# Expert weights read with eight neighbouring rows on a partition

## The reference, cut to what matters

```python
def routed_moe(x, router_w, router_b, w_gate, w_up, w_down):
    ...
    for e in range(N_EXPERTS):                       # 16
        h = jax.nn.silu(xt @ w_gate[e]) * (xt @ w_up[e])      # [512,1024] @ [1024,512]
        y = y + gates[:, e:e + 1] * (h @ w_down[e])           # [512,512] @ [512,1024]
    return y.reshape(B, S, D)
```

## Time and profile before

| | |
|---|---|
| median of 3 runs | 2137.74 us (2133.09 to 2142.99) |
| profiled execution, its own time | 2131.04 us |
| its span | 2129.4 us |
| mean granted TensorE clock | 0.945 of full |
| PE busy | 1977.8 us (93%) |
| weight loads (PEld) busy | 890.7 us (42%) |
| DVE / ACT / POOL busy | 671.2 / 402.5 / 82.1 us |
| moved by DMA | 335.56 MB in 140634 packets |

### The profile page before, as it was taken

How to read it: one execution, slowest core, us unless ns; L and a number is a source line. 1 busy time by engine, 2 the same in 40 slices (tenths; PEclk the granted TensorE clock), 3 DMA queues, 4 the chain that set the end, 5 groups by cost and what they waited for, 6 DMA issues and landing times.

```text
span 2129.4 us, 23221 instructions
## 1 busy us (share of the span) xinstructions
PE 1977.8 (93%) x9718; PEld 890.7 (42%) x9718; DVE 671.2 (32%) x1600; ACT 402.5 (19%) x869; POOL 82.1 (4%) x106
## 2 busy tenths in 40 slices
PE   7999999999999998997997999998999898899998
PEld 3454444444444444543544332333644445333322
DVE  4736312223200312105525100005586645200005
ACT  3213011111100013006501111112116421111112
POOL 0000010000000000000000200010000000200001
PEclk9989999999999999997796999999898997899999
DMA  4104542221212212201044899993110233699995
GB/s 156 60 21 142 193 159 79 79 79 69 79 40 79 79 53 79 79 4 37 1 150 152 295 399 398 396 393 138 40 40 1 80 132 145 193 397 396 397 386 206
DMA packets 140634, 335.56 MB, mean 158 GB/s; under 512 B 4537, under 2 KB 12745, under 8 KB 140401
## 3 DMA queue, kind: packets, MB, share of 16 engines
q1 hardware_dynamic: 126384, 283.80, 36.7%
q0 software_dynamic: 10976, 37.76, 4.7%
q10 hardware_dynamic: 3168, 12.50, 1.4%
HBM read 310.94 MB, written 23.09 MB: 157 GB/s over the span
## 4 chain that ended last, share of the span: by engine, by line
PE 79%; issue 8%; DMA 6%; DVE 5%; ACT 2%; POOL 0%; DVEq 0%; another core or an unknown queue 0%; ACTq 0%; POOLq 0%; SPq 0%
PE psum L580 32%; PE psum L978 20%; PE psum L823 7%; DMA ring<-in_moe_w_up 5%; PE psum L760 5%; PE psum L889 3%; PE psum L917 2%; PE psum L902 2%; PE psum L1072 1%; PE psum L959 1%; PE psum L702 1%; PE psum L592 1%; ACT ring L1429 1%; PE psum L1003 0%; PE psum L1095 0%
## 5 line engine op out<-in xcount | busy, mean ns | idle before, releaser
L978 PE MATMUL psum<-ring,scratch 128*32 128x512 f32 x3840 | 513.9, 602 | 14.4 <-DMA ring<-in_moe_w_up 11.4
L580 PE MATMUL psum<-xT,ring 128*128 128x512 f32 (+2 forms) x1056 | 466.1, 602 | 8.6 <-PE psum L580 3.4
L580 PEld LDWEIGHTS psum<-xT,ring 128*128 128x128 f32 (+2 forms) x1056 | 199.6, 191 | 272.5 <-issue 271.6
L978 PEld LDWEIGHTS psum<-ring,scratch 128*32 128x32 f32 x3840 | 142.5, 111 | 300.2 <-issue 296.0
L580 PE MATMUL psum<-ring,xT 128*128 128x512 f32 (+4 forms) x704 | 242.5, 501 | 2.5 <-ACTq L1181 1.6
L580 PEld LDWEIGHTS psum<-ring,xT 128*128 128x128 f32 x704 | 123.0, 199 | 120.1 <-issue 111.9
L823 PE MATMUL psum<-ring,scratch 128*128 128x512 f32 x352 | 155.7, 603 | 4.0 <-remote 3.3
L1591 DVE SCALAR_TENSOR_TENSOR scratch<-psum,overlay,scratch 128x511 f32<-128x511 f32 x88 | 65.9, 749 | 232.1 <-ACT scratch L1360 230.5
L978 PE MATMUL psum<-xT,scratch 128*32 128x512 f32 x768 | 129.1, 602 | 8.4 <-DMA ring<-in_moe_w_up 8.4
L2128 DVE TENSOR_TENSOR scratch<-psum,scratch 128x512 f32<-128x512 f32 x24 | 16.6, 692 | 335.9 <-PE psum L978 335.9
L823 PEld LDWEIGHTS psum<-ring,scratch 128*128 128x128 f32 x352 | 67.4, 193 | 91.6 <-issue 91.6
(11 more groups left out here) (374 smaller groups left out, 1647.3 us busy)
## 6 DMA issues: line engine op xcount, KB each, us to landing
ring<-in_moe_w_gate SPq DMA_DIRECT2D x28, 2048.0 KB, 15.1
ring<-in_moe_w_up SPq DMA_DIRECT2D x28, 2048.0 KB, 18.5
ring<-in_moe_w_down SPq DMA_DIRECT2D x24, 2048.0 KB, 16.0
ring<-in_w_up SPq DMA_DIRECT2D x11, 2048.0 KB, 7.9
xT<-in_moe_w_down SPq DMA_DIRECT2D x8, 2048.0 KB, 11.6
expert_rows<-scratch ACTq DMA_DIRECT2D x20, 512.0 KB, 7.5
ring<-in_w_down SPq DMA_DIRECT2D x4, 2048.0 KB, 7.7
ring<-in_even_w_in SPq DMA_DIRECT2D x4, 2048.0 KB, 7.7
```

The lines of the kernel that those rows point to most:

```text
L580: mm = nc.tensor.matmul(out_, lhsT, rhs, start=(j == 0), stop=(j == len(pairs) - 1))
L978: mm = nc.tensor.matmul(bank[r, :], lhsT[:, t, r], w_[:, t, c0:c0 + 512], start=(t == 0), stop=(t == nk - 1))
```

## The change

A partition now holds neighbouring rows of an expert's matrix: for gate and up partition p holds rows 8 p to 8 p + 7, for down rows 4 p to 4 p + 3. That is one unbroken piece of 16 KB in DRAM and in the buffer, and the load is written with two dimensions (128 x 4096) instead of three. The bytes in a buffer are read as before, [partition, k, n]; product k now takes the rows 8 p + k. So the turned operand must hold column 8 p + k of x on partition p: transpose k of `turn_x` reads every eighth element of a row (32 bytes apart), from k on, and transpose k of `turn_h` every fourth element of `hid` (16 bytes apart). Number, order and engine of all instructions, and all waits, stay as they were. The path for tokens beyond an expert's 96 places (`overflow`) keeps the old layout in both its loads and its transposes.

```diff
--- before.py
+++ after.py
@@ -953,11 +953,12 @@
                 mm.then_inc(idx_mm, 1)
 
             def turn_x(l, g):
+
+                of_partition = xg[:, g % 2, :].rearrange("q (p k) -> q k p", k=KD)
                 pe.wait_ge(gathered[g % 2], 16 * (NG // 2 * l + g // 2 + 1))
                 for h in range(2):
                     for t in range(4):
-                        mm = nc.tensor.transpose(banks[h][:, t * P:(t + 1) * P],
-                                                 xg[:, g % 2, (4 * h + t) * P:(4 * h + t + 1) * P], ident)
+                        mm = nc.tensor.transpose(banks[h][:, t * P:(t + 1) * P], of_partition[:, 4 * h + t, :], ident)
                     mm.then_inc(xgT_done, 1)
 
             def weights_of(l, m, g):
@@ -998,9 +999,10 @@
                     tiled(banks[5 + j], hidT, 4, views, j * 512).then_inc(y_done, 1)
 
             def turn_h(l, g):
+                of_partition = hid.rearrange("q (p k) -> q k p", k=4)
                 pe.wait_ge(h_ready, NG * l + g + 1)
                 for t in range(4):
-                    mm = nc.tensor.transpose(banks[4][:, t * P:(t + 1) * P], hid[:, t * P:(t + 1) * P], ident)
+                    mm = nc.tensor.transpose(banks[4][:, t * P:(t + 1) * P], of_partition[:, t, :], ident)
                 mm.then_inc(hT_done, 1)
 
             def share_late(l):
@@ -2532,7 +2534,7 @@
 
             def load_experts(l):
                 c0 = first_expert_chunk[l]
-                views = {m: w[n][l].rearrange("e (k p) n -> e p k n", p=P) for m, n in zip(("gate", "up", "down"), EXPERT_W)}
+                views = {m: w[n][l].rearrange("e (p k) n -> e p (k n)", p=P) for m, n in zip(("gate", "up", "down"), EXPERT_W)}
                 for m, e, b, freed in loads_of[l]:
                     if freed:
                         m_, g = freed
@@ -2548,7 +2550,8 @@
                         if b < 2:
 
                             sp.wait_ge(met, meets_through("odd_d" if l else "even_b"))
-                    sp.dma_start(expert_buffer(b, 4 if m == "down" else KD), views[m][e]).then_inc(expert_loaded[b], 16)
+
+                    sp.dma_start(expert_buffer(b, 1)[:, 0, :], views[m][e]).then_inc(expert_loaded[b], 16)
 
             for at, c in static:
                 if at < first_expert_chunk[0]:
```

## The result

| | before | after |
|---|---|---|
| median | 2135.41 us (2130.12 to 2142.99, 4 runs) | 2109.39 us (2109.26 to 2114.14, 4 runs) |
| ratio after / before | | 0.9881, 95% interval 0.9846 to 0.9916 |
| profiled execution, its own time | 2131.04 us | 2114.14 us |
| its span | 2129.4 us | 2111.2 us |
| mean granted clock | 0.945 | 0.946 |

Ratios are taken over the runs and differ a little from the quotient of two medians.) In the set of the first four experiments one execution of the kernel before took 7725.52 us: its median of 2147.21 us over 13 runs counts it, the ratios don't. The changed kernel is 1.2% faster, where no measurable difference was forecast. 2109.39 us lies just under the low end of the range, 2110. PE is busy 2 us longer than before, where 32 more for the transposes, less 5 for slow passes, were forecast.

What follows compares the result with a forecast made beforehand. PE was taken to bound the expert stages, with DMA close beside it. Transposes +32 us and vanished waits -25 us made +7: 2131.04 us becomes 2138, or 2145 against the median; range 2110 to 2160 us.

Steps and rivals of the forecast that it cites:

- What bounds the kernel: Expert stages: PE binds with DMA close; anything added to PE adds time, and loads give only their six waits.
- The price of the waits: PE's six waits for up matrices: 19.8 us standing still plus 5.2 us slow passes, 25.0 us to win.
- The loads: Expert weight loads in 16 KB pieces: DMA for three groups falls from 71.2 to 67.2 us, 69.3 if cut.
- The packet account: DMA engine time in the expert stages, reckoned as 7.3 ns a packet plus 37.4 us a MB.
- rival 1: Strided transposes cost TensorE nothing, PE keeps 67.4 us for three groups: -25 to -21, 2113 to 2117 us; chance 0.27.
- The gathers: Gathers' packets alternate with longer load pieces: 4 us more each, covered by one group of slack, costed at nothing.
- The transposes: Strided transposes on PE's critical path in expert stages: 117 ns more each, 272 of them, +32 us.
- The reading of line 702: Float32 product loads, 132-byte step: 57 ns apart, halves overlapping, so 114 ns per 64 columns; 220 taken for 128.
- lower bound: Strided transposes: nothing more if line 702's halves do not overlap or a transpose has room for the step.
- Rival 2: Weight load and transpose run in series, both paid in full: 227 ns x 272 = +62, net +37, 2175 us; chance 0.16.
- Rival 3: Transposes' loads slow from a faster rate: some 60 ns more each, +16 - 25 = -9, 2129 us; chance 0.12.
- The signs: Trace marks expected: eight loads 1.7 us, turns 1.9 and 1.0, no load waits, 12288 weight packets, beat 71 to 72.

Runs made afterwards that it cites:

- the first four experiments: Against the kernel before: new strided transposes with old loads, 2142.05 us; new loads with old transposes, 2117.44 us; added transposes at several steps; added products at several steps.
- the first experiment: Changed kernel with the old loads of 2 and 4 KB pieces put back, strided transposes kept: 2142.05 us, ratio 0.9989 to the kernel before.
- the second experiment: Changed kernel with the old transposes of neighbouring columns put back, 16 KB loads kept: 2117.44 us, ratio 0.9860 to the kernel before.

## Why the prediction was wrong

**What bounds the kernel: right for the changed one.** There PE binds, and the loads could give only their six waits. With the old loads it is not so that whatever is added to PE is added to the time: DMA needs 71.2 us for three groups and PE 67.4, and in the first experiment the slower turns came out of the waits (13.6 us for 19.8) and cost nothing that could be measured.

**The price of the waits, 25.0 us: right.** Both parts went, the 19.8 us of standing still and the 5.2 of slow passes at a granted clock of 0.50. The stages shortened by 22.7 us. With the turns' real price of 22 x (0.07 + 0.09) = 3.5 us, the sum should have been 25.0 - 3.5 = 21.5.

**The loads: right.** The packet account gave 71.2 us of DMA for three groups before and 67.2 after. One packet a partition of a matrix it is: the whole run has 140634 - 71002 = 69632 packets fewer, exactly the 81920 - 12288 of the prediction. From 1236 to 1260 us the account asks for (938 x 0.0073 + 10.22 x 37.4) / 16 = 24.3 us, and they were moved in 24. The 4 KB pieces, named under rival 1 as leaving half of the waits, left 5.7 us of the 13.6 that the old loads have with turns of about that length. That the loads alone remove every wait is shown by the second experiment.

**The gathers: right.** 4 us more were estimated, 7.7 became 11.2 (stores 7.5, then 11.0), and after the first group of a layer none waited for its gather.

**The transposes: wrong, and with them the sign.** The failed step is "A transpose is then 220 ns behind the last instead of 103: 117 ns more". Measured are 111 ns in `turn_x` (103 before) and 117 in `turn_h` (93 before): 8 and 24 more, 3.5 us in all instead of 32. The reading of line 702 behind it held up (57 ns apart for halves in turn, 245 for 128 columns), but that line is a float32 product. The prediction carried its rate over to another kind of instruction, and the clause in its own lower bound, by which a transpose "loads each column once and not twice as a float32 product does", pointed at the kind of instruction, though not at the size: even one load record against another it is 62 ns for 111. The rows to weigh it with were in the trace: neighbouring columns in a transpose start 0.103 us apart, and the moving side has the same pace, so the row gives only an upper bound for the load, which may be far quicker. I took it for the load's own rate, and took its nearness to the 107 ns worked out under rival 1 for agreement; the load of a transpose takes 62.

**The rivals.** Rival 1 is what happened: "PE keeps 67.4 us a three groups against 67.2 of DMA", 2113 to 2117 for a profiled execution of 2131.04 less 21 to 25; such an execution took 2114.14. Against the median before, 2137.74, the same terms are 2112.7 to 2116.7, and 2109.39 was measured. The medians of the result differ by 26.0 us, where the terms give 21.5; the rest stays open. Rival 1 had been given a chance of 0.27, the forecast 0.45. Rival 2's mechanism did not appear: a load of 119 ns and a transpose of 109 paid one after the other would be 228 ns, and the slowest pace of a transpose measured is 122. Rival 3's half price, 60 ns, is some five times the 13 ns (3.5 us over 272) that were measured. The low end of the range was set 3 us under rival 1, less than the scatter of the runs themselves, 5 us after and 13 before; that 2109.39 lies just outside it and not inside is chance, the wrong price is not.

**The signs.** Eight loads were to take 1.7 us and took 0.97. Turns were to take 1.9 and 1.0 us and took 1.09 and 0.68. No wait for a load and no slow passes were forecast, and there are none. A beat of 71 to 72 us was forecast, and it is 67.9. "I am wrong if the turns keep their 1.02 us (rival 1)": they did, within 0.07.

## What to carry to other kernels

Bound an operand's step by rows of the same kind of instruction: a rate read from products doesn't hold for transposes, and a row in which the load is hidden tells only how long it is at most. Where a stage's DMA time lies a few per cent above that of the bounding engine, count packets before bytes: at 7 ns for each packet, going from 2 KB to 8 KB pieces turned six waits into none. When the layout that a load likes has to be matched elsewhere, put the stride on an operand whose load hides behind moving columns.

## What the runs showed of the hardware

- Float32 weight loads at the full clock, 128 columns: 111 ns in a product, 62 in a transpose (on 32 and 64 partitions). At a step of 8 bytes 119 and 118, of 16 bytes 245 and 119, of 32 bytes 249 and 110. In a product the doubling comes at 16 bytes, in a transpose at 8, and in neither does it grow further (up to 44 bytes in a transpose, 122 ns). Why a transpose's load is the quicker stays open.
- At a granted clock of 0.50 a product's load of 128 neighbouring columns takes 213 ns, twice its 111 at 1.00, while with a step of 16 bytes it takes 233 (245 at 1.00). Line 702's indifference to the clock is thus a trait of strided loads; loads of neighbouring columns in a product don't share it.
- A queue's long packets hold up the short ones of others: with 16 KB pieces a 512 KB store lands after 11.0 us instead of 7.5, and a gather after 11.2 instead of 7.7. With 4 KB pieces they take 7.3 and 7.7, with 8 KB 8.8 and 9.1 (1240 to 1380 us).
